# Four modulation steps move from the gated recurrence into the first input projection

## What is computed

```
m    = silu(c) @ mod_w + mod_b                  # two rows: latent, context; six parts of 1024 per layer
u    = rms_norm(x, gain) * (1 + scale) + shift  # parts 1 and 2 of layer 0 are needed first
z    = u @ w_in                                 # 1024 x 2336: q, k, v, z of the recurrence, low-rank gate, heads
o    = gla_bidirectional(q, k, v, g)            # gated linear attention, both directions
...                                             # attention, output projection, experts, five more layers
```

## Time and profile before

| | us |
|---|---|
| median of 3 runs | 2087.35 (2083.67 to 2092.35) |
| the profiled execution: its time | 2086.19 |
| the profiled execution: its span | 2084.4 |
| PE / DVE / ACT busy in the span | 1767.0 / 1192.6 / 986.1 |

### The profile page before, as it was taken

The page is one execution under the profiler, slowest core; times in us unless marked ns, Lnnn a source line. Parts: engine busy times, 40 slices in busy tenths (PEclk is TensorE's granted clock), DMA queues, the critical chain, the costliest instruction groups (busy, mean ns, idle before and its releaser), DMA issues.

```text
span 2084.4 us, 25455 instructions
## 1 busy us (share of the span) xinstructions
PE 1767.0 (85%) x9896; PEld 1388.1 (67%) x9934; DVE 1192.6 (57%) x1977; ACT 986.1 (47%) x1763; POOL 100.6 (5%) x135
## 2 busy tenths in 40 slices
PE   5996878993899956897999998978899779989977
PEld 2774446772677745666899996756677458668645
DVE  2107674435698857754566666346644754563384
ACT  4223114624688855554344434435455436445463
POOL 0000100002000021100000002000000000000000
PEclk8997888997899988998999998988999989999999
DMA  7224895012999972102455553430055124325301
GB/s 298 81 110 186 316 344 219 1 61 97 361 421 422 421 286 100 42 1 81 162 181 182 191 191 130 175 120 1 30 185 180 41 85 168 122 91 181 142 1 41
DMA packets 52694, 335.94 MB, mean 161 GB/s; under 512 B 5488, under 2 KB 5488, under 8 KB 18160
## 3 DMA queue, kind: packets, MB, share of 16 engines
q1 hardware_dynamic: 46112, 310.04, 39.6%
q0 software_dynamic: 6480, 24.50, 3.1%
HBM read 305.16 MB, written 29.36 MB: 160 GB/s over the span
## 4 chain that ended last, share of the span: by engine, by line
PE 65%; DVE 15%; ACT 9%; DMA 6%; issue 4%; POOL 1%; DVEq 0%; SPq 0%; POOLq 0%; ACTq 0%
PE bank L1222 17%; PE bank L1224 16%; PE bank L1223 16%; DMA ring_float<-weights_dram 5%; DVE ring_float32r L2031 2%; ACT hT_float L722 2%; ACT arena_float L776 1%; PE bank L1419 1%; PE bank L1256 1%; PE bank L1382 1%; ACT ring_high L675 1%; PE bank L1545 1%; PE bank L1593 1%; PE bank L1537 1%; DVE stat L2698 1%
## 5 line engine op out<-in xcount | busy, mean ns | idle before, releaser
L2031 DVE TENSOR_TENSOR ring_float32r<-ring_float,ring_high 128x1024 fp32r<-128x1024 f32 x298 | 355.2, 1230 | 369.4 <-ACT ring_high L675 369.4
L675 ACT ACTIVATE ring_high<-ring_float 128x1024 fp32r<-128x1024 f32 x298 | 301.2, 1059 | 414.3 <-DMA ring_float<-weights_dram 412.6
L1222 PE MATMUL bank<-ring_high,x_float32r 128*128 128x512 f32 x608 | 243.0, 400 | 6.4 <-DVE mix_float32r L2060 3.0
L1224 PE MATMUL bank<-ring_high,mix_float32r 128*128 128x512 f32 x608 | 240.9, 396 | 0.0
L1223 PE MATMUL bank<-ring_float32r,x_float32r 128*128 128x512 f32 x608 | 240.9, 396 | 0.0
L1222 PE MATMUL bank<-ring_high,arena_float32r 128*128 128x512 f32 (+1 forms) x368 | 140.1, 381 | 18.7 <-DVE arena_float32r L2060 6.2
L1222 PE MATMUL bank<-Z_float32r,ring_high 128*128 128x256 f32 x512 | 146.0, 285 | 7.9 <-issue 4.2
L1223 PE MATMUL bank<-Z_float32r,ring_high 128*128 128x256 f32 x512 | 146.1, 285 | 0.0
L1224 PE MATMUL bank<-Z_float32r,ring_float32r 128*128 128x256 f32 x512 | 146.0, 285 | 0.0
L1382 PE MATMUL bank<-dense 128*128 128x512 bf16 x378 | 114.6, 403 | 35.9 <-ACT arena_float L1189 17.2
L1222 PEld LDWEIGHTS bank<-ring_high,x_float32r 128*128 128x128 f32 x608 | 115.9, 191 | 35.5 <-ACT hT_float L722 5.7
(11 more groups left out here) (405 smaller groups left out, 3441.1 us busy)
## 6 DMA issues: line engine op xcount, KB each, us to landing
ring_float<-weights_dram SPq DMA_DIRECT2D x234, 1024.0 KB, 4.8
Z_float<-weights_dram SPq DMA_DIRECT2D x33, 1024.0 KB, 8.6
sent<-post_row SPq DMA_DIRECT2D x1, 11776.0 KB, 37.8
Z_float<-sent SPq DMA_DIRECT2D x23, 512.0 KB, 9.0
made<-mix_float POOLq DMA_DIRECT2D x23, 512.0 KB, 7.9
post_row<-norm_post_dram POOLq DMA_DIRECT2D x4, 512.0 KB, 4.4
small<-small_dram SPq DMA_DIRECT2D x1, 1072.0 KB, 10.2
x_float<-x_dram SPq DMA_DIRECT2D x1, 1024.0 KB, 5.6
```

The lines of the kernel that those rows point to most:

```text
L675: nc.scalar.activation(ring_high[:, slot, half], ring[:, slot, half], ACT.Copy).then_inc(high_ready, 1)
L1222: nc.tensor.matmul(out, left[0], right[0], start=start, stop=False)
L1224: return nc.tensor.matmul(out, left[1], right[0], start=False, stop=stop)
L2031: ve.tensor_tensor(ring_low[:, slot, half], ring[:, slot, half], ring_high[:, slot, half], ALU.subtract).then_inc(low_ready, 1)
```

## The change

Four late modulation steps (`MOD_BETWEEN`) now run inside the first input projection. A half of a step follows each of its first eight chunks, so the ring's order there becomes in0[0], m0, in0[1], m1, ..., in0[7], m7, in0[8] (m0 to m7 are the eight halves). ACT copies the bank of a step after the drains of a block. `MOD_LEVEL` falls to 2, and in a level a step follows only the second and the fourth `pair_products`: of 13 steps left, levels 1 to 6 have two each, and level 7 has one. The diff, cut to its core:

```diff
-MOD_GATES, MOD_START, MOD_LEVEL = 1, 2, 3
+MOD_BETWEEN = 4
+MOD_GATES, MOD_START, MOD_LEVEL = 1, 2, 2
...
+IN0_AT = [STREAM["in0"][0] + 2 * c for c in range(9)]
...
-    w += chunks_of(np.concatenate([ev[:, 0:1536], ev[:, 1568:2336]], 1))
-    w += mod[2 * MOD_EARLY:]
+    in0 = chunks_of(np.concatenate([ev[:, 0:1536], ev[:, 1568:2336]], 1))
+    for c in range(2 * MOD_BETWEEN):
+        w += [in0[c], mod[2 * MOD_EARLY + c]]
+    w += [in0[8]] + mod[2 * MOD_EARLY + 2 * MOD_BETWEEN:]
...
                     if first is not None and w == 512 and start + SLOTS == made < n_chunks:
 
-                        chunk_high(first + made)
+                        chunk_high(at(made))
                         made += 1
...
-                    projected(columns(zs[0], NT, [512, 512, 512, 512, 256]), STREAM["in0"][0])
+                    projected(columns(zs[0], NT, [512, 512, 512, 512, 256]), STREAM["in0"][0],
+                              after=lambda n, t: mod_copy(mod_rows_late, int(t == NT - 1 and n < MOD_BETWEEN)))
...
+            def mod_half(rows, kh):
+
+                w = chunk().rearrange("p (k n) -> p k n", k=4)
+                if kh == 0 and mod_steps[0] not in (0, MOD_EARLY):
+                    mod_turn(rows)
...
                             chunk_done(i)
+                        if after_chunk:
+                            after_chunk(n, k0 // rows_per)
...
-                            if (d, s) != (0, 0):
+                            if s == 1:
                                 mod_late(1)
...
-                    project("first", NT, [(NT, 512)] * 4 + [(NT, 256)])
+                    project("first", NT, [(NT, 512)] * 4 + [(NT, 256)],
+                            after_chunk=lambda n, kh: mod_half(mod_rows_late, kh) if n < MOD_BETWEEN else None)
```

More of the change, by code:

```diff
@@ L121 @@
 STREAM, N_LOADS = fields(
-    [("mod_early", 2 * MOD_EARLY), ("in0", 9), ("mod_late", 2 * (MOD_STEPS - MOD_EARLY)), ("out0", 4),
+    [("mod_early", 2 * MOD_EARLY), ("in0", 9 + 2 * MOD_BETWEEN), ("mod_late", 2 * (MOD_STEPS - MOD_EARLY - MOD_BETWEEN)), ("out0", 4),
      ("experts0", len(RING_CHUNKS)),
@@ L730, in projected @@
                 n_chunks = sum(w // 256 for _, _, w in blocks)
+                at = (lambda c: first + c) if first != STREAM["in0"][0] else (lambda c: IN0_AT[c])
                 start, made = 0, SLOTS
@@ L907, in first_layer @@
                 modulate(i, 0, NT, "first")
-                chunks_high(STREAM[f"in{i}"][0] + 1, SLOTS - 1)
+                for c in range(1, SLOTS):
+                    chunk_high(IN0_AT[c] if i == 0 else STREAM[f"in{i}"][0] + c)
                 if i == 0:
-                    projected(columns(zs[0], NT, [512, 512, 512, 512, 256]), STREAM["in0"][0])
+                    projected(columns(zs[0], NT, [512, 512, 512, 512, 256]), STREAM["in0"][0],
+                              after=lambda n, t: mod_copy(mod_rows_late, int(t == NT - 1 and n < MOD_BETWEEN)))
                     drain((lrT, lambda b: b[:, :], 1.0, None))
@@ L1247, in mod_turn @@
                 return i
[L1249 to L1259, removed]
+            def mod_half(rows, kh):
+                w = chunk().rearrange("p (k n) -> p k n", k=4)
+                if kh == 0 and mod_steps[0] not in (0, MOD_EARLY):
+                    mod_turn(rows)
+                for k in range(4):
+                    i = nc.tensor.matmul(mod_bank[32 * k:32 * k + 2, :], cond[:, 4 * kh + k, :], w[:, k, :],
+                                         start=(kh == 0), stop=(kh == 1), tile_position=(0, 32 * k))
+                if kh == 0:
+                    chunk_done(i)
+                    return
                 mod_steps[0] += 1
@@ L1262, in mod_step @@
                 tenancy[-1][1:] = [mod_full, mod_steps[0]]
+            def mod_step(rows):
+                for kh in range(2):
+                    mod_half(rows, kh)
             def mod_early():
@@ L1285, in transposes, with project @@
                     i.then_inc(a_full, 1)
-            def project(name, T, blocks, between=None):
+            def project(name, T, blocks, between=None, after_chunk=None):
                 hT = split_views(name, T)
@@ L2630, in first_layer @@
                 features_low("first", NT)
-                chunks_low(first + 1, SLOTS - 1)
+                for c in range(1, SLOTS):
+                    chunk_low(IN0_AT[c] if i == 0 else first + c)
                 if i == 0:
-                    chunks_low(first + SLOTS, 9 - SLOTS)
+                    for c in range(SLOTS, 9):
+                        chunk_low(IN0_AT[c])
                     gla()
```

## The result

| | median us | lowest to highest | runs | against before |
|---|---|---|---|---|
| before | 2082.36 | 2076.64 to 2092.35 | 11 | |
| changed | 2097.47 | 2090.99 to 2107.87 | 11 | 1.0068, 95% interval 1.0047 to 1.0089 |

The change costs 14 us (0.0068 x 2082), with an interval of 9.8 to 18.5. The forecast was +19, with a range of +7 to +32 around the 2087 of the time: slower by more than 0.5%, as predicted, and a little less than predicted. The profiled execution took 2090.99 (span 2089.2) and is the fastest of its eleven. So the verdict comes from the medians, and the profile only tells where the time lies.

What follows compares the result with a forecast made beforehand. The prediction took PE to bound the projection and late modulation loads the levels. Projection +45.9, levels -27 and start of `gla()` +0.5 made about +19 us, 2087.35 to 2106, range 2094 to 2119.

Steps and rivals of the forecast that it cites:

- The order of the borders: Projection, ends of blocks 0 to 2: PE stalls as ACT's high part awaits its load before the drains; +29.7 us.
- five steps of the chain: At each such border: half ends, load 6.5 us, high part 1.9, four drains 2.1, PE start 0.25; sum 10.8.
- The load: Projection borders: chunk 2n+3's load, issued behind another, taken as 6.5 us, bounds 4.8 and 7.3.
- The clock: Projection, after each idle stretch at a border: next block begins slow, 2.1 us each, +6.3 in all, bounds 3 and 7.
- The work: Projection: added halves and three turns on PE's path, 10.8 us, less 0.9 as m7 covers block 3's border wait.
- Projection in all: Whole projection: 10.8 - 0.9 + 29.7 + 6.3 = +45.9 us.
- The levels: Levels 1 to 6, 12 steps in place of 17: 109.6 us falls to about 82.5, gain 27, bounds 34 and 22.
- The waits between them: Levels 1 to 6: late loads add 0.9 us a level to DVE's 75.7, plus 1.5 for a low-clock start.
- The loads hide: Rival, borders of blocks 0 to 2: PE finds its banks drained, so no stall; -17 us, 2070; chance 0.07.
- The levels gain less: Rival, levels: each removed step is worth only PE's work, 5 x 3.0 = 15 us; +31, 2118; chance 0.13.
- All that DVE allows and short borders: Rival: levels gain 34 us and border loads take 4.8 us; about +7, 2094; chance 0.10.

Runs made afterwards that it cites:

- drains first: The changed kernel, but in the projection ACT makes the high part of chunk 2n+3 behind block n's drains, not ahead; 2061.40 us, 0.9897 of the kernel before.
- filler: The changed kernel with 44 dense bf16 matmuls on PE ahead of each of projection blocks 1 to 3; 2097.47 us, 1.0055 of the kernel before.
- Seventeen left out: The kernel before with all 17 modulation steps of the levels left out (loads, matmuls, copies); 2049.22 us, 0.9828 of the kernel before.

## Why the prediction held, point by point

- **The order of the borders.** All five steps of the chain are in the trace as they were put: m1, a load issued behind another (6.20 to 6.28, forecast 6.5), the high part and the drains (2.00 and 1.95 on the chain, forecast 1.9 and 2.1), the start. The stall is 10.49 to 10.57 against 10.8. Experiment "drains first" shows the cause: with the same bytes and the same ring, a change in ACT's order alone takes it away.
- **The load.** The trace has 6.2 us for a load behind another one, so the row that was taken (6.5) held. The Trainium skill ("DMA: Bandwidth & Descriptors", section "Anatomy of one DMA — SWDGE (gpsimd) path") led to an estimate of 4.4 us and to +13 for the change. Its fit is for one transfer on the path of GpSimd, and these loads are issued by SP, one behind another. At this term the trace doesn't agree. That +13 lies near the measured +14 is an accident: the levels gave 7.7 us more than the sum had for them.
- **The clock.** 4.4 us at 0.50 behind each stall were forecast; it was 4.2 behind the first and about 4 behind the others (a mean of 0.54 over 4.4 us and of 0.58 over 4.7). The price, 2.1 a border, was 1.8 at each of the three (12.3 less a stall of 10.5), and the filler shows the same 1.8 at two of them.
- **The work.** Forecast 10.8 less one border's 0.89. In "drains first", where the work stands alone, it is 7.5: all four halves m1, m3, m5 and m7 lie over such a gap (10.8 - 4 x 0.89 = 7.2), not only m7. In the change three of these gaps are inside the stall, which I had counted as 10.8 less 0.89, so the sum was the same.
- **Projection in all.** Work 7.5, stalls 31.6, clock 5.4, less the 1.0 us by which the change was faster than "drains first" ahead of m1: 43.5, measured 43.4. The prediction had 45.9 and no term for the last; why the change met the full clock sooner there no run shows.
- **The levels: the mis-sized term.** Forecast -27, measured -34.7 (-32.5 against the second profile of the kernel before). The step that was off is "The waits between them": 0.9 a level and 1.5 for a slow start, 6.9 us on top of DVE's 75.7. DVE's work itself was right (forecast 75.7, 76.66 in the trace). Its waits for PE were 0.4 us in all, so the low clock of level 1 cost it nothing either. The loads were late as said (PE waited 6.3 us for them at the halves), but I had charged their delay to DVE one for one. DVE has the decay and the head work between its pairs, and I read the 0.4 as PE catching up during these; no run isolates it. Levels 1 to 6 took 77.8, not 82.5, and the end 13.3, not 16.2 with up to 3 on top: DVE has 11.28 us of work in it where the earlier trace rows had 14.85, so less of its work is left when level 7 begins. "Seventeen left out" shows that hardly more was to be had (1.6 us). One reading was wrong, without effect on the sum: PE waits for what comes into a freed slot three positions later, not two.
- **Rivals.** *The loads hide* needed a border under 5.5 us; it was 12.3. "Drains first" is the kernel that this rival describes: -17 forecast, -21 measured (0.9897). *The levels gain less* fell with L1 to L7 at 77.8. *All that DVE allows and short borders* was right in its first half.
- **The start.** The prediction had nothing there; it is +2.2 us (below).

In total, the errors are -2.5 in the projection, -7.8 in the levels and the end, +2.2 at the start: 19 - 8 = 11 by stages. The misses of the levels and of the start have opposite signs, and that helped the time. The measured 14 us (9.8 to 18.5) can't tell these from the rest's variation.

## What to carry to other kernels

Before an item is put into a ring of slots, write down for each load of the ring which instruction frees its slot now, and then look at what stands behind that load's first consumer in the consumer's own list. Here the moved work was nearly free (7.5 us for a gain of 34.7); one high part that stood ahead of four drains made it a loss, and one condition made it a gain of 1.0%. When a stage has two limits close together, take out work only down to the crossing: the step from three to two a level was worth 19 us and that from two to none 1.6.

## What the runs showed that I had not expected

- Every edited kernel starts its projection 1.1 to 2.7 us later than the kernel before, even those in which nothing ahead of the projection has changed. In the change all of the 2.2 us are there when the early modulation steps end: the first transposes behind them are at 36.10 before and at 38.33 in the change. A part of it is the clock. The last turn of these steps, with a window around it, in the kernel before:

```profile
35.19 1.05 PE L1246 MATMUL bank<-const,scratch 128*128 128x2 f32 x8 [0.73 <-ACT scratch L651]
...
34.00:36.00 2.00, 1.27 (x12) 0.81 (x9) 0.00 (x0) 0.60 (x1) 0.00 (x0) 1.00 0.93 332
```

  and in the change:

```profile
36.60 1.87 PE L1253 MATMUL bank<-const,scratch 128*128 128x2 f32 x8 [0.72 <-ACT scratch L655]
...
36.00:38.00 2.00, 1.40 (x7) 1.40 (x7) 0.00 (x0) 0.55 (x1) 0.00 (x0) 0.50 0.98 397
```

  The same instructions, at the same place, after the same wait, at a granted clock of 1.00 and of 0.50. The first turn differs in the same way (1.02 us before, 1.84 in the change), but there the profile has a granted clock of 1.00 in both kernels, so that its cause stays open. Why one program gets the full clock there and the other doesn't was not settled.
- A gap of 2.18 us between filler and block was followed by a stretch at 0.50 later in the block, where gaps of 0.93 and 0.84 were not.
- The rest of the kernel, 1750 to 1770 us of identical work, differs by up to 17 us from one profiled execution to another, more than the change is worth.
